# Latent attention layers: rotary tiles in iterations of their own, gates elsewhere, first output steps beside the last pairs

## The reference

```python
x = _layernorm(DEEPNORM_ALPHA * x + y, ln_g[i], ln_b[i])
```

```python
o = _dense_causal(q_full, k_full, v, scale).reshape(B, S, MLA_WIDTH)
return (o * jax.nn.silu(gate)) @ w_out
```

## Time and profile before

| | |
|---|---|
| median of three runs | 2081.78 us |
| profiled execution | 2081.22 us |
| its span | 2079.4 us |
| mean granted TensorE clock | 0.932 |
| TensorE busy | 1842.2 us (89%) |
| VectorE busy | 839.8 us (40%) |
| ScalarE busy | 778.4 us (37%) |
| GpSimd busy | 596.1 us (29%) |

### The profile page before, as it was taken

How to read it: one execution, slowest core, us unless ns; L and a number is a source line. 1 busy time by engine, 2 the same in 40 slices (tenths; PEclk the granted TensorE clock), 3 DMA queues, 4 the chain that set the end, 5 groups by cost and what they waited for, 6 DMA issues and landing times.

```text
span 2079.4 us, 23634 instructions
## 1 busy us (share of the span) xinstructions
PE 1842.2 (89%) x9152; PEld 1448.3 (70%) x9152; DVE 839.8 (40%) x1831; ACT 778.4 (37%) x1556; POOL 596.1 (29%) x291
## 2 busy tenths in 40 slices
PE   7888888999869999898888897978779899999978
PEld 6666666776748888576655576767647688788767
DVE  2545536476333344533555516467452211100141
ACT  4444443465134444513444433323243423212242
POOL 4321122232233232114311121233101444444422
PEclk9998898999989999998999997798899899999989
DMA  5211133288533222123211133122102333233311
GB/s 145 52 34 39 52 111 106 71 80 76 121 87 82 62 62 64 39 81 85 50 34 45 49 122 103 51 71 61 51 21 71 91 95 98 91 95 94 112 55 71
DMA packets 214794, 154.98 MB, mean 75 GB/s; under 512 B 54107, under 2 KB 197227, under 8 KB 214684
## 3 DMA queue, kind: packets, MB, share of 16 engines
q1 hardware_dynamic: 205072, 128.37, 22.0%
q10 hardware_dynamic: 9308, 24.83, 7.1%
q0 software_dynamic: 304, 0.28, 0.1%
HBM read 144.38 MB, written 8.91 MB: 74 GB/s over the span
## 4 chain that ended last, share of the span: by engine, by line
PE 60%; DVE 13%; ACT 5%; issue 2%; ACTq 1%; POOL 1%; DMA 0%; POOLq 0%; DVEq 0%
PE banks L446 18%; PE banks L448 17%; PE banks L447 17%; DVE AB L1828 2%; PE banks L556 2%; PE banks L598 1%; PE banks L622 1%; ACT AB L1209 1%; PE banks L545 1%; DVE AB L1924 1%; PE banks L637 1%; PE banks L606 1%; DVE AB L1922 1%; DVE QKl L1651 1%; DVE AB L1915 1%
## 5 line engine op out<-in xcount | busy, mean ns | idle before, releaser
L2241 POOL TENSOR_TENSOR w_lo<-w_raw,w_hi 128x1024 fp32r<-128x1024 f32 (+3 forms) x255 | 583.9, 2295 | 1451.8 <-ACT w_hi L1078 1451.8
L446 PE MATMUL banks<-XTh,w_hi 128*128 128x512 f32 (+1 forms) x1088 | 445.2, 409 | 19.1 <-DVE XTl L1871 7.6
L447 PE MATMUL banks<-XTl,w_hi 128*128 128x512 f32 (+1 forms) x1088 | 432.4, 397 | 0.0
L448 PE MATMUL banks<-XTh,w_lo 128*128 128x512 f32 (+1 forms) x1088 | 432.1, 397 | 0.0
L1078 ACT ACTIVATE w_hi<-w_raw 128x1024 fp32r<-128x1024 f32 (+3 forms) x255 | 253.2, 1001 | 245.1 <-PE banks L448 173.8
L446 PEld LDWEIGHTS banks<-XTh,w_hi 128*128 128x128 f32 x1088 | 209.5, 193 | 74.1 <-issue 20.7
L448 PEld LDWEIGHTS banks<-XTh,w_lo 128*128 128x128 f32 x1088 | 208.4, 192 | 46.4 <-issue 1.4
L447 PEld LDWEIGHTS banks<-XTl,w_hi 128*128 128x128 f32 x1088 | 209.3, 192 | 43.0 <-issue 2.6
L446 PE MATMUL banks<-w_hi,OTh 128*128 128x512 f32 (+1 forms) x448 | 173.7, 388 | 13.3 <-POOL w_lo L2241 5.0
L447 PE MATMUL banks<-w_lo,OTh 128*128 128x512 f32 (+1 forms) x448 | 170.8, 381 | 0.0
L448 PE MATMUL banks<-w_hi,OTl 128*128 128x512 f32 (+1 forms) x448 | 170.5, 381 | 0.0
(11 more groups left out here) (199 smaller groups left out, 2764.4 us busy)
## 6 DMA issues: line engine op xcount, KB each, us to landing
w_raw<-in_w_gate_up_dram SPq DMA_DIRECT2D x44, 512.0 KB, 3.8
w_raw<-in_fox_w_in_dram SPq DMA_DIRECT2D x32, 512.0 KB, 4.0
w_raw<-in_mla_w_in_dram SPq DMA_DIRECT2D x26, 512.0 KB, 3.9
w_raw<-in_w_in_dram SPq DMA_DIRECT2D x24, 512.0 KB, 3.8
w_raw<-in_w_down_dram SPq DMA_DIRECT2D x22, 512.0 KB, 3.5
w_raw<-in_swa_w_in_dram SPq DMA_DIRECT2D x20, 512.0 KB, 3.9
w_raw<-in_mla_w_out_dram SPq DMA_DIRECT2D x16, 512.0 KB, 3.6
w_raw<-in_mla_w_kv_up_dram SPq DMA_DIRECT2D x32, 128.0 KB, 2.8
```

What stands on the lines that cost most here:

```text
L446: nc.tensor.matmul(o, ah, bh, start=first, stop=False, skip_group_check=True)
L447: nc.tensor.matmul(o, ah, bl, start=False, stop=False, skip_group_check=True)
L448: return nc.tensor.matmul(o, al, bh, start=False, stop=last, skip_group_check=True)
L2241: pool.tensor_tensor(view(w_lo, u, RING), view(w_raw, u, RAW), view(w_hi, u, RING).bitcast(F32), ALU.subtract).then_inc(lo_done, 1)
```

## The change

In both latent layers the units come in another order, and with them the tiles on all engines. Rotary tile 1 moves to the setup, 2 and 3 to iterations 0 and 2, alone at position 1. Gates 2 to 7 move to iterations -1, 1, 3, 4, 5, 6. All queries move to position 2, ahead of the keys. On VectorE the rotary work of iterations 0 and 2 comes between the first and second maxima. On ScalarE, in all pair layers, position 1 comes between the two halves of the exponentials. `out_ahead` is called three times in every pair layer: step 0 after mix of iteration 6, steps 1 and 2 at position 1 of iteration 7, woven with the turns.

```diff
+MLA_GATE = {-1: 2, 1: 3, 3: 4, 4: 5, 5: 6, 6: 7}
@@ plan_units
         query(1)
+        rope(1)
         for i in range(-1, 7):
-            if i % 2:
-                if i < 5:
-                    rope((i + 3) // 2)
-                    query(i + 3)
-                    if i < 0:
-                        gate(2)
-                    keys_values((i + 3) // 2)
-                else:
-                    gate(6)
-            else:
-                gate((3, 4, 5, 7)[i // 2])
-                if i < 6:
-                    query(i + 3)
+            if i in MLA_GATE:
+                gate(MLA_GATE[i])
+            if i in (0, 2):
+                rope(i // 2 + 2)
+            if i < 5:
+                query(i + 3)
+            if i in (-1, 1, 3):
+                keys_values((i + 3) // 2)
@@ TensorE, pair_attention
                     woven.append(next_step)
                     fill(i, 1)
+                    if i == n_pairs - 1 and ahead:
+                        ahead(1)
+                        ahead(2)
                     woven.pop()
...
                     scores(i + 2, 2)
-                    if i == n_pairs - 1 and ahead:
-                        ahead()
                     mix(i)
                     fill(i, 3)
+                    if i == n_pairs - 2 and ahead:
+                        ahead(0)
@@ TensorE
-            def out_ahead(name, src):
+            def out_ahead(name, src, k):
 
                 pe.wait_ge(ps_free, c.sch)
-                pe.wait_ge(po_lo, c.pair + 1)
+                pe.wait_ge(po_lo, c.pair + k + 1)
                 begun.append(unit(name))
                 for t in range(2):
-                    row_step(0, t, src, begun[0], True, False)
+                    row_step(k, t, src, begun[k], k == 0, False)
+                    weave()
@@ TensorE, out_rows
-                    ahead = bool(begun)
+                    ahead = k < len(begun)
...
-                        if ahead and t == 2:
+                        if paired and k == 0 and t == 2:
                             pe.wait_ge(pt_free, c.tch)
-                        if ahead and t == T - 1:
+                        if paired and k == 0 and t == T - 1:
                             groups_stored(pe, c.g)
@@ TensorE, fill of a latent layer (ScalarE and VectorE alike)
+                            rope(1)
...
+                    elif pos == 1:
+                        if i in MLA_GATE:
+                            tile("gate")
+                        if i in (0, 2):
+                            rope(i // 2 + 2)
+                    elif pos == 2:
+                        if i < 5:
                             query(i + 3)
+                        if i in (-1, 1, 3):
+                            keys((i + 3) // 2)
+                    elif pos == 3 and i in (-1, 1, 3):
+                        vals((i + 3) // 2)
@@ ScalarE, pair_attention
                         early()
+                    fill(i, 1)
                     exps(i + 1, 1)
-                    fill(i, 1)
                     fill(i, 2)
@@ VectorE, pair_attention
                     maxima(i + 2, 0)
+                    if rotary(i):
+                        fill(i, 1)
                     maxima(i + 2, 1)
                     norm(i + 1, 0)
-                    fill(i, 1)
+                    if not rotary(i):
+                        fill(i, 1)
                     norm(i + 1, 1)
```

More of the change, by code:

```diff
@@ L718, in out_rows @@
                 for k in range(n - held):
-                    ahead = bool(begun)
+                    ahead = k < len(begun)
                     if paired:
                         pe.wait_ge(po_lo, c.pair - KD + k + 1)
-                    part = begun.pop() if ahead else unit(name)
+                    part = begun[k] if ahead else unit(name)
                     for t in range(T):
@@ L733, in out_rows @@
                     return
+                begun.clear()
                 if paired:
@@ L852, in fill @@
                             query(1)
+                            rope(1)
                             pe.wait_ge(kr_done, 7 * (j + 1))
[L854 to L857, removed]
-                            query(i + 3)
[L859 to L868, removed]
+                    elif pos == 1:
[5 more added lines that the diff above has]
+                        if i < 5:
+                            query(i + 3)
+                        if i in (-1, 1, 3):
+                            keys((i + 3) // 2)
+                    elif pos == 3 and i in (-1, 1, 3):
+                        vals((i + 3) // 2)
                 def src(k, ts):
                     return OTh[:, MLA_OUT[k], ts], OTl[:, MLA_OUT[k], ts]
-                pair_attention(mla_pairs(), fill, lambda: out_ahead("out", src))
+                pair_attention(mla_pairs(), fill, lambda k: out_ahead("out", src, k))
                 out_rows("out", KD, src, turned=(lambda t: HT) if j else (lambda t: x_tok[:, t, :]), lag=2 if j else 1)
@@ L905, in fill @@
                     tile("gate")
-            pair_attention(swa_pairs(), fill, lambda: out_ahead("out", of(OTh, OTl)))
+            pair_attention(swa_pairs(), fill, lambda k: out_ahead("out", of(OTh, OTl), k))
             out_rows("out", KD, of(OTh, OTl), turned=lambda t: x_tok[:, t, :])
@@ L1407, in fill @@
                             query(1)
[L1408 to L1411, removed]
-                            query(i + 3)
[L1413 to L1424, removed]
+                            rope(1)
+                    elif pos == 1:
+                        if i in MLA_GATE:
+                            advance()
+                            gate(MLA_GATE[i])
+                        if i in (0, 2):
+                            rope(i // 2 + 2)
+                    elif pos == 2:
+                        if i < 5:
+                            query(i + 3)
+                        if i in (-1, 1, 3):
+                            keys((i + 3) // 2)
+                    elif pos == 3 and i in (-1, 1, 3):
+                        vals((i + 3) // 2)
                 pair_attention(mla_pairs(), fill)
@@ L1779, in _, with pair_attention @@
             gate_at = {}
-            def pair_attention(pairs, fill):
+            def pair_attention(pairs, fill, rotary=lambda i: False):
                 a0, n_pairs = c.pair, len(pairs)
@@ L2003, in fill @@
                             query(1)
+                            rope(1)
                             if j:
                                 dve.wait_ge(x_out, 16 * T * 2)
[L2006 to L2009, removed]
-                            query(i + 3)
[L2011 to L2025, removed]
+                    elif pos == 1:
+                        if i in MLA_GATE:
+                            gate(MLA_GATE[i])
+                            gate_at[MLA_GATE[i]] = c.g
+                        if i in (0, 2):
+                            rope(i // 2 + 2)
+                    elif pos == 2:
+                        if i < 5:
+                            query(i + 3)
+                        if i in (-1, 1, 3):
+                            keys((i + 3) // 2)
+                    elif pos == 3 and i in (-1, 1, 3):
+                        c.g += 2
+                pair_attention(mla_pairs(), fill, lambda i: i in (0, 2))
                 ln_tail(3 * j)
```

## The result

The changed kernel takes 2089.76 us, the median of 17 runs (2084.51 to 2094.72), against 2080.67 (2076.8 to 2085.09, 17 runs) before: ratio 1.0043, 95% interval 1.0034 to 1.0053. It is slower by 9 us where 10 us faster was forecast, and outside the range, which ended at 2085. The profiled execution is one of 2089.76 us, span 2087.9, mean granted clock 0.924 where it was 0.932.

The account below looks back on a forecast made before the run. Bound by TensorE's matmul work, its gaps and its low clock. Tails 4.0+1.8, window layer 0 and loops 4.2 sum to 10.0 us: 2081.2-10.0 = 2071.2, said as 2071; range 2050 to 2085, the forecast's own 2064 to 2078.

Parts of the forecast that it names:

- The tails: Output steps beside the last pairs of the latent layers: 4.0 us won in the first, 1.8 in the second.
- The window layer: ScalarE's queue still holds step 3's weight split, so TensorE arrives 5 us earlier and waits 5 us longer: 0.
- The idle time of the loops: Latent loops, per layer: new waits of 20.3 us against 21.3 us of gaps removed.
- second norm's last scaling: Iteration 1 of the latent loops: taken as not held by GpSimd's pass; if held, 2.5 us longer there.
- The rule that the prediction used: VectorE and GpSimd share an exclusive port lock; whoever starts first keeps it; if not so, 5.0 us worse, 2076.
- The clock: Latent loops: 10 us per layer lost in dips before; less 1.5 and 4x1.7 leaves 1.7, 1.1 kept as gain.
- the 6.29 gaps: TensorE's four waits of 6.29 us for VectorE's rotary product, iterations 1 and 3 of each latent layer; expected to go.
- ScalarE's order: Fill 1 before the second exponentials in all pair layers: 0; without the gate tile's cover, 2 us an iteration.
- C: Slower: late second exponentials push norms into GpSimd's next pass, 2.4 held plus 2.1 dip per case; 2089, chance 0.12.
- A: Rotary stalls really go and new gaps halve, +10 per layer: 2055, with the window tail 2050; chance 0.20.
- B: Tails bring nothing, weights being the bound, and the loop is even; 2 us left in all: 2079, chance 0.20.
- The profile's sign that I gave for a failure: Wrong if gaps in iterations 0 to 3 sum to under 12 us a layer, or window w_lo wait stays 5.

## Why the prediction was wrong, step by step

**The tails: right in the first layer, too low in the second.** Forecast 4.0 and 1.8 us, measured 4.3 and 3.35. Half of the 7.65 us is idle time (2.8 and 1.0 less). The other half is busy time: iterations 6 and 7 had lost 2.1 and 4.5 us to the low clock and now lose none. The forecast walked the new iteration 7 at full-clock pace against a measured old one, so it held this gain without naming it. In the first layer mix(7) waits 0.84 for the last copies, as walked through, and TensorE waits 0.68 for w_lo once; in the second it waits 2.54 for w_lo, where I had 3.4.

```profile
317.94 0.50 PE L443 MATMUL banks<-w_hi,OTh 128*128 128x512 f32 x1 [0.68 <-POOL w_lo L2237]
...
1250.10 0.76 PE L443 MATMUL banks<-w_hi,OTh 128*128 128x512 f32 x1 [2.54 <-POOL w_lo L2237]
```

**The window layer: right.** Forecast 0, measured 0.2 slower, w_lo's wait up from 4.80 to 8.31 with the end unmoved.

**The idle time of the loops: right in sum.** I forecast new waits of 20.3 for 21.3 removed, 1.0 less. Up to the first turn of iteration 6 idle time fell by 2.0 and 2.5. The norm beside the kv weights' pass took what the earlier trace rows said, 3.37 us with a pass of 2.34:

```profile
136.08 3.37 DVE L1825 TENSOR_SCALAR AB<-AB,ri 128x128 f32<-128x128 f32 x4
...
136.82 2.34 POOL L2237 TENSOR_TENSOR w_lo<-w_raw,w_hi 128x1024 fp32r<-128x1024 f32 x1 [1.60 <-ACT w_hi L1078]
```

In iteration 1 I had taken the second norm's last scaling as not held. That was wrong. The norm began at 161.52 and took 4.15 us, through a pass of 1.07 from 161.61 and one of 2.35 from 163.03: its second scaling, from 161.72, and its fourth, from 163.08, were held. It cost little: the wait that was to be 1.5 came as 1.88.

The prediction asked whether a scaling that has begun is held by a pass that begins after it, and left it open. The traces answer it. Of the kernel before:

```profile
136.20 0.29 DVE L1828 TENSOR_SCALAR AB<-AB,ri 128x128 f32<-128x128 f32 x1
136.40 2.45 DVE L1828 TENSOR_SCALAR AB<-AB,ri 128x256 f32<-128x256 f32 x1
...
136.31 2.39 POOL L2241 TENSOR_TENSOR w_lo<-w_raw,w_hi 128x1024 fp32r<-128x1024 f32 x1 [2.43 <-ACT w_hi L1078]
```

The first scaling began 0.11 us ahead of the pass and took 0.29 us, as without one; the second began 0.09 behind it and was held to its end. So it is in every norm of the traces of before and after: 70 scalings that began from 0.03 to 0.32 us ahead of a pass took their usual 0.3 to 0.5 us, and each of the 81 that began during a pass was held to its end, the one of the earlier trace rows though it began only 0.01 us behind it. The rule that the prediction used holds; what it had wrong was the order of the two starts in iteration 1, where the pass came 0.05 us first.

**The clock: the step that failed.** The sentence was "dips after the 6.29 gaps ran 4.3 us each; of the new gaps I expect four dips at about 1.7". I counted dips by gaps and priced each like the one of the earlier trace rows. But the new gaps stand in clusters: 0.87, 2.15 and 0.90 within eleven microseconds, then, eighteen later, 2.33 and 1.88. After the first of these the clock was low for 10.2 us on end, nearly all of it on work. The prediction had 10 us lost to the clock in each loop before and 8.9 after. Up to iteration 6 the loops had in fact lost 10.8 and 6.4 before (the 12.9 and 10.9 above hold 2.1 and 4.5 of iteration 7 as well), so the 10 was too much for the second layer; and after, it was 18.1 and 20.1, all of it ahead of iteration 6. So the clock took 7.3 and 13.7 us more, where 1.1 less was forecast, and the idle time 2.0 and 2.5 less, which makes 5.3 and 11.2 longer where 4.3 and 9.9 were measured. The dips removed were worth little: much of their low clock ran out while TensorE was idle (3.7 of 6.8 us at the gap that ended at 211.07). The prediction had each layer's loop 2.1 us shorter, 1.1 of it from the clock. The runs with spare matmuls show the cause: same order, TensorE at work in its waits, clock nearly full, 27 us less.

The Trainium skill (TensorE: Matmul & The Clock Gate, "HAM oscillation — how this bites in real kernels") describes waits between bursts of matmuls that put the clock down again and again, so that each burst begins slow. The traces agree on the pattern: 0.57 over 140 to 152 behind the cluster, 1.00 there with the gaps filled. They differ in size: each wait in that section's example is longer than any in this cluster, of which the longest is 2.15 us, and here the short ones were enough; on that the measurement decides.

**ScalarE's order: priced at 0, which no run contradicts for the new order of tiles.** In the old order the same line cost 9 us; in the new one the difference, 1.0038 against 1.0043, is within noise.

**The rivals.** C had the number (2089), with a chance of 0.12, and not the cause, so its number is luck: it was to come from further norms held by passes, with the dip as an addition. VectorE's scalings in all took 131.0 us over the kernel, 136.9 before, so they were held less, not more. A and B did not happen. The profile's sign that I gave for a failure (gaps under 12 us, or the window layer's wait staying at 5) could not catch it, as it looked at idle time only.

**What stays open.** That closeness of gaps makes the difference is read from the traces; no run moved the same gaps apart. And it is no full rule: the gaps of 2.33 and 1.88 at 160 us left only 3.4 us of low clock, the like ones of the second layer 6.8, and the gaps of 0.87 and 3.03 of iteration 6 none. What the runs do show is that working through the gaps brings the clock and the time back.

The second latent loop lost 9.9 and the first 4.3, from starting points that differ: before, the second one had lost 10.9 us to the clock and the first 12.9. Runs of the changed kernel had mean clocks from 0.924 to 0.930 and times from 2094.72 to 2084.51, so part of this difference may be one execution's luck; the loops of other executions were not measured. The setup of the first layer, from the end of the wait at 65 us to vals(0), was 1.5 us longer in this profile, but nearly 1 us longer also in that of the output steps alone, which do not touch it.

## What to carry to other kernels

- Where TensorE is busy for most of the time, count for a reordering the work done at low clock, not the idle time alone. Here gaps of 0.87, 2.15 and 0.90 us close together cost as much as one of 6.29, because the low clock then fell on work.
- If a gap can't be closed, real work moved into it (the output steps: 5 us) or spare matmuls in it (11 us in these loops, from 0.9972 to 0.9919 of 2080, and 12 more in the norm tails) keep the clock. A run with the spare work is also the test of whether an order is bad in itself.
- Price a change to the queue order of one engine by what stands second in the queue afterwards, in every iteration; one moved line cost 9 us in the old order of tiles.

## What the runs showed of the hardware that was not expected

- Spare matmuls with a 128-column fp32 result took 0.24 us each (24 instructions for 12 of them in 2.92 us), and with them the granted clock of the first loop rose from 0.89 to 0.99. With one in each gap it stayed at 0.57 in the stretch after the cluster.
- The low stretches of the changed kernel's loops differed much in length: 3.4 us behind a single gap of 1.74, 3.4 to 13.7 us behind pairs of gaps of 1.6 to 3.1, and 10.2 us behind each of the four clusters of three.
- A VectorE scaling was held by every GpSimd pass that had begun before it, even by 0.01 us (2.61 us instead of 0.48), and by none that began 0.03 us or more after it.
